# Chunked delta scan: first masks beside the gates, query norms by one-column products, banks exchanged, sums of squares moved

## The reference, cut to what matters

```python
q = l2norm(q) * DK ** -0.5          # per token and head; q has 4 heads of 128
k = l2norm(k)
# per head and chunk, forward and on reversed tokens:
v_new = u_c - w_c @ s
o_c   = qd_c @ s + qk_c @ v_new     # qd = q * exp(g), qk = (q k^T) * exp(g_i - g_j), masked
s     = s * dl_c + ke_c.T @ v_new
# afterwards
o = rmsnorm(o_f + rev(o_b), o_norm_w) * silu(gate)
```

## Time and profile before

| what | value |
|---|---|
| median of 3 runs | 1594.7 us |
| the three runs | 1594.7, 1595.63, 1586.18 us |
| the profiled execution | 1596.06 us, its span 1594.2 us |
| mean granted TensorE clock | 0.986 of full speed |
| PE busy | 1535.2 us (96%) |
| DVE, ACT, POOL busy | 935.2, 477.2, 398.4 us |
| share of the chain that ended last | PE 84%, DVE 4%, ACT 3%, DMA 3%, POOL 2% |

### The profile page before, as it was taken

The page is one execution under the profiler, slowest core; times in us unless marked ns, Lnnn a source line. Parts: engine busy times, 40 slices in busy tenths (PEclk is TensorE's granted clock), DMA queues, the critical chain, the costliest instruction groups (busy, mean ns, idle before and its releaser), DMA issues.

```text
span 1594.2 us, 24076 instructions
## 1 busy us (share of the span) xinstructions
PE 1535.2 (96%) x9816; PEld 1477.7 (93%) x9816; DVE 935.2 (59%) x1407; ACT 477.2 (30%) x833; POOL 398.4 (25%) x204
## 2 busy tenths in 40 slices
PE   5899999999999998999999999999999999999997
PEld 1789999999988988998999999999999999999996
DVE  2743453569978885336885266527643673467257
ACT  4322244231156665225221032121212210222024
POOL 0011111570124343130241124113212321223120
PEclk9799999999999999999999999999999999999998
DMA  9454223632427447110111111111111111111103
GB/s 348 165 197 155 100 79 116 188 110 80 150 95 236 129 140 263 40 66 1 40 53 40 41 41 40 45 49 40 40 40 41 41 53 40 41 40 40 40 1 119
DMA packets 74640, 142.87 MB, mean 90 GB/s; under 512 B 19228, under 2 KB 44900, under 8 KB 72868
## 3 DMA queue, kind: packets, MB, share of 16 engines
q1 hardware_dynamic: 70932, 134.00, 24.8%
q10 hardware_dynamic: 3168, 5.51, 0.9%
q0 software_dynamic: 432, 1.77, 0.3%
HBM read 120.60 MB, written 20.65 MB: 89 GB/s over the span
## 4 chain that ended last, share of the span: by engine, by line
PE 84%; DVE 4%; issue 3%; ACT 3%; DMA 3%; POOL 2%; SPq 0%; DVEq 0%; ACTq 0%; POOLq 0%
PE ps L2249 49%; PE ps L2251 24%; PE ps L1062 4%; DMA araw<-wts 2%; PE ps L2190 2%; PE ps L2200 1%; POOL wL L1173 1%; PE ps L2454 1%; DVE fa L2084 1%; DMA q<-q_d 0%; PE ps L1007 0%; DVE TT L917 0%; PE ps L2317 0%; POOL gbA L1183 0%; DVE X L1971 0%
## 5 line engine op out<-in xcount | busy, mean ns | idle before, releaser
L2249 PE MATMUL ps<-hH,wH 128*128 128x384 f32 x1680 | 567.9, 338 | 7.8 <-DVE hL L1688 3.6
L2251 PE MATMUL ps<-hL,wH 128*128 128x384 f32 x1680 | 563.2, 335 | 0.0
L1173 POOL TENSOR_TENSOR wL<-raw,wH 128x1024 fp32r<-128x1024 f32 x93 | 226.7, 2438 | 892.5 <-ACT wH L1364 892.1
L2249 PE MATMUL ps<-hH,wL 128*128 128x384 f32 x1680 | 382.5, 335 | 0.0
L2249 PEld LDWEIGHTS ps<-hH,wH 128*128 128x128 f32 x1680 | 316.8, 189 | 15.9 <-issue 13.1
L1364 ACT ACTIVATE wH<-raw 128x1024 fp32r<-128x1024 f32 x99 | 105.1, 1062 | 714.9 <-PE ps L2249 713.9
L2251 PEld LDWEIGHTS ps<-hL,wH 128*128 128x128 f32 x1680 | 316.8, 189 | 0.0
L2084 DVE SCALAR_TENSOR_TENSOR fa<-G,cst,fa 128x1024 f32<-128x1024 f32 x176 | 296.3, 1684 | 15.4 <-DVE fa L2081 0.6
L2249 PEld LDWEIGHTS ps<-hH,wL 128*128 128x128 f32 x1680 | 300.3, 188 | 0.0
L2249 PE MATMUL ps<-pH,wH 128*128 128x384 f32 x528 | 179.4, 340 | 4.1 <-DVE pL L2108 1.9
L1971 DVE SCALAR_TENSOR_TENSOR X<-ps,mod,X 128x384 f32<-128x384 f32 x138 | 70.5, 567 | 187.3 <-PE ps L2249 187.3
(11 more groups left out here) (308 smaller groups left out, 1864.2 us busy)
## 6 DMA issues: line engine op xcount, KB each, us to landing
raw<-wts SPq DMA_DIRECT2D x103, 512.0 KB, 3.3
araw<-wts SPq DMA_DIRECT2D x48, 512.0 KB, 6.0
X<-xT SPq DMA_DIRECT2D x8, 1152.0 KB, 13.7
kv<-tok_d SPq DMA_DIRECT2D x16, 512.0 KB, 4.8
tok_d<-stage ACTq DMA_DIRECT2D x18, 256.0 KB, 2.0
q<-q_d SPq DMA_DIRECT2D x18, 256.0 KB, 5.7
gb<-grow_d SPq DMA_DIRECT2D x18, 256.0 KB, 3.5
y<-X SPq DMA_DIRECT2D x8, 384.0 KB, 2.4
```

Of the source, the lines that this page charges most:

```text
L1173: nc.gpsimd.tensor_tensor(weight(1, u4), raw[:, u4 % RAW, :], weight(0, u4).bitcast(F32), ALU.subtract).then_inc(s["wl_ready"], 1)
L2249: last = M(out, lhs, rh[:, c], start=(k == 0 and not lo), stop=(lo and k == kts - 1))
L2251: M(out, lhs, rl[:, c], start=False, stop=False)
```

## The change

- The directions exchange their banks. Forward uses 4 to 7, backward 0 to 3. PE waits for the last gate block's banks only before `with_state(1, 0)`.
- The first tile's masks (POOL) go beside the second gate block, its exponentials (ACT) beside the third, and its decayed queries (POOL) beside the third. Its R stands in slot 0 of `raw` and its qd in `gb0`. Units 32 and 33, for which slot 0 and 1 are needed, are therefore loaded in the first scan step, behind the queries of tile 1.
- ACT squares the queries from SBUF, key-major. PE then multiplies each squared 128x128 tile by one column of ones, four products, into four columns of bank 3. DVE copies the four columns.
- The sums of squares of the output go from before `z_copy` to the end of the DVE step, and `log_mean` and `root` go from before the outputs to the end of the ACT step, behind `corner`. In the last step both stay where they were. `closing` goes behind `with_state(1)`, except in the last step.

```diff
     def bank_of(d):
-        return range(4 * d, 4 * d + 4)
+        return range(4 - 4 * d, 8 - 4 * d)
...
+    def R_of(d, y):
+        return dl[d]["R"][:] if y else dl[d]["R0"]
+    def qd_of(d, y):
+        return dl[d]["qd" if y else "gb0"]
...
-            for v in range(RAW + 8, U_OUT + 1 + RAW):
+            for v in range(RAW + 8, U_OUT + 3):
                 after_split(N_ADA + v, v, 0)
...
                     if d == 0:
-                        sp.wait_ge(s["trq"], y)
+                        sp.wait_ge(s["q_sq"], y)
                     sp.dma_start(b["q"][:], q_d[:, :, t * P:t * P + P]).then_inc(s[f"q_in_{d}"], 16)
                 if y == 1:
+                    seen(sp, "pt", 1, 1)
+                    for v in range(U_OUT + 3, U_OUT + 1 + RAW):
+                        after_split(N_ADA + v, v, 0)
...
+        def masked(pool, d, y):
+            landed_at(pool, "gb_in", d, y + 1)
+            seen(pool, "pt", d, y)
+            tri = cst[:, C_TRI + P * d:C_TRI + P * d + P]
+            done(nc.gpsimd.tensor_tensor(R_of(d, y), gb_raw(d, y)[:], per_head(tri), ALU.add), "r_mask")
+        def decayed(pool, d, y):
+            seen(pool, "gb_exp", d, y + 1)
+            landed_at(pool, "q_in", d, y + 1)
+            done(nc.gpsimd.tensor_tensor(qd_of(d, y)[:], gb_raw(d, y)[:], q_of(d, y)[:], ALU.mult), "q_decayed")
...
+        def exps(y):
+            act, A = nc.scalar, nc.scalar.activation
+            for d in range(2):
+                t = tile_of(d, y)
+                seen(act, "r_mask", d, y + 1)
+                for h in range(H):
+                    last = A(R_of(d, y)[:, h, :], R_of(d, y)[:, h, :], ACT.Exp, bias=SC[:, t, d, NG + h:NG + h + 1])
+                done(last, "r_exp")
+            if y < LAST:
+                for d in range(2):
+                    done(A(gb_raw(d, y)[:], gb_raw(d, y)[:], ACT.Exp), "gb_exp")
+        def query_squares(act, y):
+            landed_at(act, "q_in", 0, y + 1)
+            act.wait_ge(s["trq"], y) if y else act.wait_ge(s["solved"], 3)
+            nc.scalar.activation(qsq, q_of(0, y)[:], ACT.Square).then_inc(s["q_sq"], 1)
...
+                if x == LAST:
+                    for d, t, i in summed(x):
+                        log_mean(d, i)
+                    for d, t, i in summed(x):
+                        root(d, i)
+                if 0 < y < TT_:
+                    query_squares(act, y)
...
-                if y < TT_:
-                    act.wait_ge(s["trq"], y + 1)
-                    if y:
-                        act.wait_ge(s["q_sum"], y)
-                    A(qsq, heads(bank_of(0)[3]), ACT.Square).then_inc(s["q_sq"], 1)
...
                 if 0 < y < TT_:
                     corner(y)
+                if x < LAST:
+                    for d, t, i in summed(x):
+                        log_mean(d, i)
+                    for d, t, i in summed(x):
+                        root(d, i)
...
                 if pre:
                     weights(1, y)
-                    for d, t, i in summed(x):
-                        sum_squares(d, t, i)
...
                 if pre:
-                    dve.wait_ge(s["q_sq"], y + 1)
-                    V.tensor_reduce(ssq[:, tile_of(0, y), :], qsq, mybir.AxisListType.X, ALU.add).then_inc(s["q_sum"], 1)
+                    dve.wait_ge(s["trq"], y + 1)
+                    V.tensor_copy(ssq[:, tile_of(0, y), :], ps[:, bank_of(0)[3], 0:H]).then_inc(s["q_sum"], 1)
                 if LAST // 2 <= x < LAST:
                     second_out(1, x)
+                if x < LAST:
+                    for d, t, i in summed(x):
+                        sum_squares(d, t, i)
...
             def query_rows(y):
                 seen(pe, "pt", 0, y + 1)
-                turn(bank_of(0)[3], lambda h: q_of(0, y)[:, h, :]).then_inc(s["trq"], 1)
+                pe.wait_ge(s["q_sq"], y + 1)
+                for h in range(H):
+                    last = M(ps[:, bank_of(0)[3], h:h + 1], qsq[:, h, :], mat("ones")[:, 0:1], start=True, stop=True)
+                last.then_inc(s["trq"], 1)
...
-                if x == 0:
-                    pe.wait_ge(side_free[(N_Z - 1) % 2], (N_Z - 1) // 2 + 1)
                 if scan and x < LAST:
                     with_state(0, x)
-                closing(x)
+                if x == LAST:
+                    closing(x)
...
                 if pre and y:
                     first_products(pe, y)
+                if x == 0:
+                    pe.wait_ge(side_free[(N_Z - 1) % 2], (N_Z - 1) // 2 + 1)
                 if scan and x < LAST:
                     with_state(1, x)
+                if x < LAST:
+                    closing(x)
...
+                if g == 1:
+                    pool.wait_ge(s["wl_ready"], w + 3)
+                    for d in range(2):
+                        masked(pool, d, 0)
+                if g == 2:
+                    for d in range(2):
+                        decayed(pool, d, 0)
...
                 if g == 2:
                     first_z(act)
                     first_values(act)
+                    exps(0)
                     corner(0)
+                    query_squares(act, 0)
```

More of the change, by code:

```diff
@@ L667, in scale @@
                 done(gp.tensor_tensor(oTok[:, t], oTok[:, t], along(b["rs"][:], P), ALU.mult), "o_scaled")
-            for x in range(-1, TT_):
+            for x in range(TT_):
                 y = x + 1
```

54 lines of the change are left out of this document (16 added, 38 removed).

## The result

The changed kernel's median is 1608.24 us (1603.89 to 1609.48, 4 runs). Beside it the kernel before ran at 1591.72 us (1586.18 to 1595.63, 4 runs). The ratio is 1.0101, with a 95% interval from 1.0061 to 1.0142: some 16 us, where +7.5 was forecast. The range ended at 1607.

What follows compares the result with a forecast made beforehand. PE was taken to hold 84% of the chain. Hand-over, first step and loads +1.6, dearer products +1.6, steps 5 to 7 +0.1, last step +4.2: +7.5 us on the 1594.7 us median, hence 1602 us, range 1591 to 1607.

Steps and rivals of the forecast that it cites:

- the +1.6 us for the hand-over, the first scan step and the two loads together: At Y(0,1): later gate rows behind the two loads absorb the hand-over's gain and x = 0's dearer products, +1.6 us in all.
- the same nothing in x = 6 and x = 7: Late steps: the main forecast gave further clock falls behind PE's pauses no cost; only a rival priced them, 1.7 us each.
- much slower: Rival: late pauses near 584 and 605 us bring clock falls, both loads count fully; +12.4 us, 1607 us, chance 0.15.
- Norms: PE-bound steps x = 1 to 4: one-column products replace transposes, +0.40 us a step, +1.6 us in all.
- the two-column row: Profile row of PE products with two columns, same loaded shape: 16 records in 1.68 us, taken as 0.105 us a record.
- Cheap columns: Rival: product cost goes with its columns, so one-column products cost next to nothing; +4.1 us, 1599 us, chance 0.10.
- Hand-over: Gate blocks to scan start: early masks bring PT and Y forward, -0.7 us, between -1.5 and +0.8.
- the gain of 0.77 us on PT: Start of the scan: PT waits only for DVE's gate block, at 473.90 instead of 474.67 us, 0.77 us earlier.
- Loads: First step, full SP queue: units 32 and 33 make the landing 1.6 us later, between 0 and +3.1.
- Steps 5 to 7: Late steps: the wait for `z_copy` goes, later roots bring a wait for Y; +0.1 us, from -4 to +3.4.
- The gain of x = 5: End of x = 5: PE no longer waits for `z_copy` behind the sums of squares, -1.2 us.
- Last step: Before step 8's solve: `closing(8)` waits for outputs scaled later, +4.2 us, between +2.0 and +5.0.

Runs made afterwards that it cites:

- e6: Kernel before with only the new query norms (ACT's square, one-column products), square ahead of logarithm and root: ratio 1.0049, stretch 156.24 us.
- e1: Changed kernel with sums of squares, logarithm and root back in their old places, ACT's query square behind logarithm and root: ratio 1.0143, stretch 179.77 us.
- e2: Changed kernel with ACT's first query square behind the last gate's hyperbolic tangent instead of ahead of it: ratio 1.0091, stretch 167.90 us.
- e13: Changed kernel cut to exchanged banks and early masks, exponentials and decayed queries, loads in the fifth preparation: ratio 1.0006 to the kernel before.
- e11: Kernel before with only units 32 and 33 loaded in the first scan step: ratio 1.0033, stretch 161.72 us.
- e12: Kernel before with only the later sums of squares, logarithm and root, and the later `closing`: ratio 1.0048, stretch 163.75 us.
- e7: Kernel before with only DVE's `z_copy` moved ahead of the sums of squares: ratio 1.0010, stretch 155.41 us.
- e10: Changed kernel with old sums places, query square before logarithm, `z_copy` first, masks before scaling, loads and first square late: ratio 1.0003 to the kernel before.
- e14: Early masks with `z_copy` first, masks ahead of scaling and `closing` behind `with_state(1)`: ratio 0.9997 to the kernel before, stretch 158.79 us.
- e8: Kernel before with unused POOL masks beside the second and third gate block, units 32 and 33 loaded in the fifth preparation: ratio 1.0026.
- e4: Changed kernel with query norms by four transposes again, ACT's square from PSUM and DVE's row sums as before: ratio 1.0080, stretch 167.74 us.
- e9: Kernel before with `z_copy` first, POOL's masks ahead of scaling, and `closing` behind `with_state(1)` except in the last step: ratio 0.9982, stretch 153.41 us.
- e3: Changed kernel with units 32 and 33 loaded in step y = 4 instead of y = 1: ratio 1.0072, stretch 167.53 us.
- e5: Changed kernel with sums of squares, logarithm and root in their old places, ACT's query square ahead of the logarithm: ratio 1.0076, stretch 165.27 us.

## Why the prediction was wrong

The step that failed is the +1.6 us for the hand-over, the first scan step and the two loads together, which with the dearer products of x = 1 makes +2.0: the three rows measured +7.9. It holds three errors: the hand-over loses 3.2 us instead of gaining 0.7, the gate rows land 2.8 us later through the loads alone and not 1.6, and the falls of the clock behind both pauses were put at nothing. The second failure is the same nothing in x = 6 and x = 7: +8.3 us for both with the last step, where +5.5 was forecast. These two are off by 5.9 and 2.8 us, the other rows by +0.2, -0.1 and -0.9.

By the chances the time fell in the neighbourhood of the "much slower" rival (1607 us, 0.15), and past it by 1.2 us. That rival was right on the falls of the clock in the late steps and nearly so on the loads; of the hand-over it knew nothing. Point by point:

**Norms: right in the PE-bound steps.** +0.40 us a step was forecast, +0.46 to 0.48 measured, and +0.45 with the norms alone. By the ratio the norms alone cost more than these steps explain (e6). At full clock the eight records take 0.81 us from their start to the next group's:

```profile
487.27 0.95 PE L1152 MATMUL ps<-cst,ptmp 128*128 128x1 f32 x8
488.08 1.14 PE L1092 MATMUL ps<-Y,PT 128*128 128x128 f32 x8
```

That is 0.10 us a record, as the two-column row said. "Cheap columns" is refuted. The 25 ns that the Trainium skill, "TensorE: Matmul & The Clock Gate", section "Back-to-back issue gap", gives as the least spacing of narrow products isn't reached here, where each product loads its own 128x128 block. What I left out: one column makes PE wait for ACT's square, where the transposes waited for nothing on ACT. "ACT reads the queries earlier; neither is the bound there, so 0" was wrong in the hand-over, of the changed kernel and of e6, and in e1's order.

**Hand-over: wrong in sign.** Forecast -0.7 (ends -1.5 and +0.8), measured +3.2, 2.0 of it the longer wait and 1.2 the dearer products, at half clock. I listed the early masks, exponentials and decayed queries, and not the first square as an instruction of ACT's queue with a wait of its own, ahead of the last hyperbolic tangent. Taking it away brought the wait back to 2.50 us (e2). POOL's sharing with DVE, which I had named as a possible delay of up to 1.5 us, is real: DVE's inverse ends 4 us later. It eats the gain of 0.77 us on PT even without the square (e13).

**Loads: right mechanism, too small.** Forecast +1.6 at Y(0,1) for the hand-over, x = 0 and the loads together, which with +0.4 for x = 1 is +2.0; measured +7.9 for the same three. The landing was put 1.6 us later, because keys and queries of tile 1 would be issued earlier. They are issued 2.1 us later against the first query product, with the whole hand-over; and the two loads alone make 2.8 us (e11), near the upper end of 3.1. I had not priced the fall of the clock behind the wait, 1.6 us, nor that the late start doesn't vanish in this wait: the gate rows' issue moved with the hand-over, by 3.15 us relative to the first mark. Alone, the loads cost 5.3 us by the ratio and 6.3 in the profiled execution (e11).

**Steps 5 to 7.** The gain of x = 5 was right, -1.3 against -1.2. The chain root, scaling, masks, exponentials, Y came as forecast. The times have to be counted from the start of x = 6, which the forecast has at 575.5 and the trace at 577.05: scaling 4.2 us behind it in the forecast and 4.0 in the trace, exponentials 7.5 and 7.3, Y 11.1 and 10.9, PE's wait 3.2 and 2.9. The forecast names only one table load, the root's; the logarithm's (L823, 577.67) came while the sums were still under way, and the logarithm began no later than forecast. What failed lies behind the wait: 9.4 us were forecast from there to x = 7, and 11.4 were measured. 1.4 of the difference are two groups of products under the low clock (1.87 and 1.52 us to the next group, where 1.00 is usual), and 0.4 the one-column products, left out there. The fall of the clock was priced only as a rival. x = 7 up to `within(1, 7)` repeats it: +1.3 us, where 0.15 was forecast.

**Last step: right.** +4.2 us forecast for the last solve, of which 0.5 came from above; +4.1 measured from the last group of `within(1, 7)` to it. The wait of 5.11 us comes from this part alone (e12).

The three parts on the kernel before, each alone, add 0.49, 0.33 and 0.48%, the early masks 0.06%: 1.36% in all against the 1.01% measured, whose interval holds 1.36. In the stretches it is 0.85 + 6.33 + 8.36 - 1.03 = 14.5 us against 15.5. The agreement is partly luck: no single part has the square ahead of the hyperbolic tangent, and the wait for Y in x = 1 with the loads in place varied from 0.70 to 4.24 us among six executions of different kernels. No part of the change is a gain by itself; that is shown for norms, loads and sums, while the early masks are at zero.

## What to carry to other kernels

When an operation moves to another queue or ahead on one, list every instruction in front of which it now stands and every event that it waits for: the 0.6 us square held PE by 2 us, because it waited for DVE and a hyperbolic tangent stood behind it. When you hold a forecast against a trace, count both from the start of the step: absolute times carry every shift that came before. Price a pause on a matrix engine with what follows it: behind the waits of 2.67 and 2.93 us the low clock cost another 1.6 and 1.4 us, so a late input cost about half again as much as its wait.

## What the runs showed of the hardware

- Falls of the clock don't follow from the length of a pause alone. Behind the pause of 2.5 us for PT the clock stayed up in the kernel before, e7, e10, e11 and e14, and behind 3.26 us in e8; it fell behind 2.5 us in e2, e4, e9, e12 and e13, in e2 for some 8 us. Behind the four pauses of 4.5 us (changed kernel, e1, e3, e5) it fell each time. Each is a single execution. What a low clock cost is read from the durations of groups; no edit controlled the clock.
- The first 60 us differ by chance: mean clock 0.74 to 0.91 between 20 and 60 us, and the first query product between 463.3 and 470.9 us in kernels whose work up to there differs in little. A single pair of profiles can hide 7.6 us so.
- DVE is held, not slowed, beside POOL's masks: 2.93 and 2.94 us for an operation of 0.42, over both of POOL's instructions. Beside the decayed queries it was held by one instruction at a time.
- Two loads of 512 KB ahead of the gate rows on a busy queue delayed their landing from 8.3 to 11.1 us behind the issue (e11); without the loads it was 8.1 again (e3).
